# A gated three-tap convolution that reads its projection from PSUM: one core, layer trunk in float32 halves

## The reference

```python
def conv_ffn(h, w_up, w_dw, b_dw, w_down):        # w_up: 1024 -> 5632, w_dw: 3 taps a channel
    a = causal_dwconv(h @ w_up, w_dw) + b_dw
    g, val = jnp.split(a, 2, axis=-1)
    return (jax.nn.silu(g) * val) @ w_down
```

## Time and profile before

| | us |
|---|---|
| runs before the change: median (lowest to highest of 3) | 1390.86 (1390.37 to 1390.91) |
| the profiled execution, its own time | 1390.45 |
| its span, first to last instruction | 1388.7 |
| TensorE busy | 1279.1 |
| VectorE busy | 970.8 |
| ScalarE busy | 568.2 |
| GpSimd busy | 556.9 |
| mean granted TensorE clock | 0.963 |

### The profile page before, as it was taken

How to read it: one execution, slowest core, us unless ns; L and a number is a source line. 1 busy time by engine, 2 the same in 40 slices (tenths; PEclk the granted TensorE clock), 3 DMA queues, 4 the chain that set the end, 5 groups by cost and what they waited for, 6 DMA issues and landing times.

```text
span 1388.7 us, 17136 instructions
## 1 busy us (share of the span) xinstructions
PE 1279.1 (92%) x5496; PEld 998.6 (72%) x5496; DVE 970.8 (70%) x1309; ACT 568.2 (41%) x873; POOL 556.9 (40%) x265
## 2 busy tenths in 40 slices
PE   4899899889989889999999999989999999999996
PEld 2666676667667667778888767746778888887885
DVE  5667777773689899888734699985288988994102
ACT  3345555453533333334212364565344454442221
POOL 1332323213234343345444267772344444544440
PEclk9799999999989999999999999999999999999998
DMA  8533233332244444422444221110222322333221
GB/s 321 198 134 107 106 121 121 114 114 76 91 165 133 141 160 142 151 88 91 156 156 172 95 91 61 61 60 0 92 73 94 106 91 91 99 96 110 84 96 60
DMA packets 44918, 156.78 MB, mean 113 GB/s; under 512 B 4936, under 2 KB 5192, under 8 KB 44880
## 3 DMA queue, kind: packets, MB, share of 16 engines
q1 hardware_dynamic: 43488, 153.98, 32.6%
q10 hardware_dynamic: 1392, 2.32, 0.5%
HBM read 154.15 MB, written 2.12 MB: 113 GB/s over the span
## 4 chain that ended last, share of the span: by engine, by line
PE 69%; DVE 16%; issue 7%; ACT 5%; DMA 2%; DVEq 0%; SPq 0%; ACTq 0%
PE psum L834 20%; PE psum L835 20%; PE psum L836 20%; PE psum L1102 3%; DVE z L1305 2%; DMA ada_first<-ada_w 2%; DVE acc_mid L1184 2%; DVE tmp L1454 2%; PE psum L845 2%; DVE tmp L1226 2%; ACT L556 1%; DVE h_lo L1230 1%; DVE acc L1184 1%; DVE pt_lo L1314 1%; PE psum L881 0%
## 5 line engine op out<-in xcount | busy, mean ns | idle before, releaser
L454 POOL TENSOR_TENSOR w_lo<-w_raw,w_hi 128x1024 fp32r<-128x1024 f32 (+1 forms) x192 | 479.1, 2511 | 776.6 <-ACT w_hi L535 776.6
L834 PE MATMUL psum<-h_hi,w_hi 128*128 128x512 f32 x1152 | 477.4, 414 | 13.7 <-DVE h_lo L1230 8.5
L835 PE MATMUL psum<-h_lo,w_hi 128*128 128x512 f32 x1152 | 460.3, 400 | 0.0
L836 PE MATMUL psum<-h_hi,w_lo 128*128 128x512 f32 x1152 | 459.5, 399 | 0.0
L834 PEld LDWEIGHTS psum<-h_hi,w_hi 128*128 128x128 f32 x1152 | 223.8, 194 | 69.9 <-DVE h_lo L1230 11.1
L836 PEld LDWEIGHTS psum<-h_hi,w_lo 128*128 128x128 f32 x1152 | 223.1, 194 | 48.8
L835 PEld LDWEIGHTS psum<-h_lo,w_hi 128*128 128x128 f32 x1152 | 222.8, 193 | 48.0 <-issue 5.3
L535 ACT ACTIVATE w_hi<-w_raw 128x1024 fp32r<-128x1024 f32 (+1 forms) x192 | 191.6, 1037 | 84.1 <-DMA w_raw<-w_tiles 84.1
L1412 DVE SCALAR_TENSOR_TENSOR x<-psum,mod,x 128x512 f32<-128x512 f32 (+1 forms) x32 | 23.3, 749 | 180.5 <-PE psum L836 180.5
L834 PE MATMUL psum<-a_hi,w_hi 128*128 128x512 f32 x352 | 139.3, 396 | 0.8 <-issue 0.8
L836 PE MATMUL psum<-a_hi,w_lo 128*128 128x512 f32 x352 | 138.9, 395 | 0.0
(11 more groups left out here) (176 smaller groups left out, 1486.2 us busy)
## 6 DMA issues: line engine op xcount, KB each, us to landing
w_raw<-w_tiles SPq DMA_DIRECT2D x160, 512.0 KB, 3.4
ada_buf<-ada_w SPq DMA_DIRECT2D x32, 512.0 KB, 3.3
ada_mid<-ada_w SPq DMA_DIRECT2D x32, 512.0 KB, 3.5
w_raw<-w_tiles SPq DMA_DIRECT2D x32, 448.0 KB, 3.2
ada_first<-ada_w SPq DMA_DIRECT2D x16, 512.0 KB, 6.1
ada_late<-ada_w SPq DMA_DIRECT2D x16, 512.0 KB, 4.2
x<-x_in SPq DMA_DIRECT2D x4, 512.0 KB, 10.1
bias<-rel_scratch ACTq DMA_DIRECT2D x1, 2048.0 KB, 8.1
```

The costliest lines, as they stand in the source:

```text
L454: nc.gpsimd.tensor_tensor(w_lo[:, slot, 0:k], w_raw[:, (ph.tile + l) % 2, 0:k], f(w_hi[:, slot, 0:k]), ALU.subtract).then_inc(lo_done, 1)
L834: nc.tensor.matmul(dst, w_hi[:, slot, k], rhs_hi, start=first, stop=False)
L835: nc.tensor.matmul(dst, w_hi[:, slot, k], rhs_lo, start=False, stop=False)
L836: return nc.tensor.matmul(dst, w_lo[:, slot, k], rhs_hi, start=False, stop=last)
```

## The change

ScalarE no longer copies the banks to padded tiles. It applies tap 2 and the bias to each bank on the way (Identity with a scale and a bias column) into tap buffers that alternate with the group: `tmp0` and `tmp1` for c = 0, the bodies of `pad_g` and `pad_v` for c = 1. VectorE adds taps 1 and 0 to them, reading shifted columns of the PSUM banks. Silu goes back into bank 2c, the product is formed there in place, ScalarE rounds it from there into `a_hi`, and VectorE subtracts from there. ScalarE's two or three splits stand between these steps. Silu's table is loaded explicitly ahead of each body. TensorE waits for `act_ready` before it uses the banks again, and the zero columns are gone.

```diff
+        taps_g = (tmp0[:], pad_g[:, 2:S + 2])
+        taps_v = (tmp1[:], pad_v[:, 2:S + 2])
...
             def up_phase(ph, then, layer):
                 def group(i, c, nxt):
+                    w = [col("ff", lin(i, 8 * (FM * layer + c) + n, 16)) for n in range(8)]
+                    m = lin(i, c, 2)
                     act.wait_ge(used, lin(i, ph.group + c + 1, 2))
-                    act.wait_ge(taps_done, lin(i, FM * layer + c + 1, 2))
-                    nc.scalar.activation(pad_g[:, 2:S + 2], psum[:, 2 * c], ACT.Copy).then_inc(pad_ready, 1)
-                    nc.scalar.activation(pad_v[:, 2:S + 2], psum[:, 2 * c + 1], ACT.Copy).then_inc(pad_ready, 1)
-                    split_group(*nxt)
+                    if not (isinstance(i, int) and i == 0):
+                        act.wait_ge(act_ready, lin(i, FM * layer + c - 1, 2))
+                    nc.scalar.activation(taps_g[c], psum[:, 2 * c], ACT.Identity, bias=w[3],
+                                         scale=w[2]).then_inc(pad_ready, 1)
+                    nc.scalar.activation(taps_v[c], psum[:, 2 * c + 1], ACT.Identity, bias=w[7],
+                                         scale=w[6]).then_inc(pad_ready, 1)
+                    slots_free(nxt[0], nxt[1], nxt[2])
+                    split_tile(nxt[0], nxt[1], nxt[0].per_group * nxt[2])
                     act.wait_ge(conv_g, lin(i, FM * layer + c + 1, 2))
-                    nc.scalar.activation(tmp0[:], tmp0[:], ACT.Silu).then_inc(silu_done, 1)
-
-                with act.Fori(0, ph.bodies - 1) as i:
+                    nc.scalar.activation(psum[:, 2 * c], taps_g[c], ACT.Silu).then_inc(silu_done, 1)
+                    split_tile(nxt[0], nxt[1], nxt[0].per_group * nxt[2] + 1)
+                    act.wait_ge(gated, lin(i, FM * layer + c + 1, 2))
+                    nc.scalar.activation(tile_of(a_hi, m), psum[:, 2 * c], ACT.Copy).then_inc(a_hi_done, 1)
+                    for j in range(2, nxt[0].per_group):
+                        split_tile(nxt[0], nxt[1], nxt[0].per_group * nxt[2] + j)
+
+                load_table(ACT.Silu)
+                for c in range(2):
+                    group(0, c, (ph, 1, c))
+                with act.Fori(1, ph.bodies - 1) as i:
+                    load_table(ACT.Silu)
                     for c in range(2):
                         group(i, c, (ph, i + 1, c))
...
             def up0_pair(i, c):
-                pe.wait_ge(pad_ready, lin(i, 2 * (c - 1), 4))
+                pe.wait_ge(act_ready, lin(i, c - 1, 2))
                 pair(UP0, i, c)
...
-            V.memset(pad_g[:, 0:2], 0.0).then_inc(taps_done, 1)
-            V.memset(pad_v[:, 0:2], 0.0).then_inc(act_ready, 1)
...
-                    V.tensor_scalar(tmp0[:], pad_g[:, 2:S + 2], w[2], w[3], ALU.mult, ALU.add)\
-                     .then_inc(dve_step, own.tick())
+                    V.scalar_tensor_tensor(out=g[:, 1:S], in0=psum[:, 2 * c, 0:S - 1], scalar=w[1], in1=g[:, 1:S],
+                                           op0=ALU.mult, op1=ALU.add).then_inc(dve_step, own.tick())
...
+                    V.scalar_tensor_tensor(out=g[:, 2:S], in0=psum[:, 2 * c, 0:S - 2], scalar=w[0], in1=g[:, 2:S],
                                            op0=ALU.mult, op1=ALU.add).then_inc(conv_g, 1)
...
-                    V.tensor_tensor(tmp1[:], tmp0[:], tmp1[:], ALU.mult).then_inc(dve_step, own.tick())
-                    dve.wait_ge(dve_step, own.now())
+                    V.tensor_tensor(psum[:, 2 * c], psum[:, 2 * c], v, ALU.mult).then_inc(gated, 1)
+                    dve.wait_ge(a_hi_done, lin(i, FM * layer + c + 1, 2))
                     m = lin(i, c, 2)
-                    V.tensor_copy(tile_of(a_hi, m), tmp1[:]).then_inc(dve_step, own.tick())
-                    dve.wait_ge(dve_step, own.now())
-                    V.tensor_tensor(tile_of(a_lo, m), tmp1[:], f(tile_of(a_hi, m)), ALU.subtract)\
+                    V.tensor_tensor(tile_of(a_lo, m), psum[:, 2 * c], f(tile_of(a_hi, m)), ALU.subtract)\
                      .then_inc(act_ready, 1)
```

More of the change, by code:

```diff
@@ L270, in trunk @@
         o_copied, o_squared, ms_read, o_inv = sem("o_copied"), sem("o_squared"), sem("ms_read"), sem("o_inv")
-        pad_ready, silu_done = sem("pad_ready"), sem("silu_done")
+        pad_ready, silu_done, a_hi_done = sem("pad_ready"), sem("silu_done"), sem("a_hi_done")
         sig_ready, prod_ready = sem("sig_ready"), sem("prod_ready")
@@ L289, in trunk @@
         conv_g, taps_done, act_ready = sem("conv_g"), sem("taps_done"), sem("act_ready")
+        gated = sem("gated")
         u_ready, y_ready = sem("u_ready"), sem("y_ready")
@@ L1046, in group @@
                             if isinstance(i, int) and i == 0 and c == 0:
-                                pe.wait_ge(act_ready, FM * layer + n + 2)
+                                pe.wait_ge(act_ready, FM * layer + n + 1)
                             last = mm3(psum[:, 2 * c], 3 * c + j, k, a_hi[:, n], a_lo[:, n], n == 0, n == FM - 1)
@@ L1052, in down @@
                 for c in range(2):
-                    pe.wait_ge(pad_ready, 2 * (FM * (layer + 1) - 1 + c))
-                    if c == 1:
-                        pe.wait_ge(act_ready, FM * (layer + 1) + 1)
+                    pe.wait_ge(act_ready, FM * (layer + 1) - 1 + c)
                     group(0, c)
@@ L1145, in _ @@
             keep_warm(18)
-            pairs(UP1, 5 * DK, pad_ready, 2 * FM, 2)
+            pairs(UP1, 5 * DK, act_ready, FM, 1)
             group = down(DOWN1, 1)
@@ L1443, in group @@
                     dve.wait_ge(pad_ready, lin(i, 2 * (FM * layer + c) + 2, 4))
-                    dve.wait_ge(act_ready, lin(i, FM * layer + c + 1, 2))
-                    V.tensor_scalar(tmp1[:], pad_v[:, 2:S + 2], w[6], w[7], ALU.mult, ALU.add)\
-                     .then_inc(dve_step, own.tick())
+                    V.scalar_tensor_tensor(out=v[:, 1:S], in0=psum[:, 2 * c + 1, 0:S - 1], scalar=w[5],
+                                           in1=v[:, 1:S], op0=ALU.mult, op1=ALU.add).then_inc(dve_step, own.tick())
@@ L1447, in group @@
                     dve.wait_ge(dve_step, own.now(back=1))
[L1448 to L1452, removed]
@@ L1453, in group @@
-                    dve.wait_ge(dve_step, own.now(back=1))
-                    V.scalar_tensor_tensor(out=tmp0[:], in0=pad_g[:, 0:S], scalar=w[0], in1=tmp0[:],
+                    V.scalar_tensor_tensor(out=g[:, 2:S], in0=psum[:, 2 * c, 0:S - 2], scalar=w[0], in1=g[:, 2:S],
                                            op0=ALU.mult, op1=ALU.add).then_inc(conv_g, 1)
                     dve.wait_ge(dve_step, own.now())
-                    V.scalar_tensor_tensor(out=tmp1[:], in0=pad_v[:, 0:S], scalar=w[4], in1=tmp1[:],
-                                           op0=ALU.mult, op1=ALU.add).then_inc(taps_done, 1)
+                    V.scalar_tensor_tensor(out=v[:, 2:S], in0=psum[:, 2 * c + 1, 0:S - 2], scalar=w[4],
+                                           in1=v[:, 2:S], op0=ALU.mult, op1=ALU.add).then_inc(taps_done, 1)
@@ L1459, in group @@
                     dve.wait_ge(silu_done, lin(i, FM * layer + c + 1, 2))
[L1460 to L1462 removed]
+                    dve.wait_ge(taps_done, lin(i, FM * layer + c + 1, 2))
+                    V.tensor_tensor(psum[:, 2 * c], psum[:, 2 * c], v, ALU.mult).then_inc(gated, 1)
+                    dve.wait_ge(a_hi_done, lin(i, FM * layer + c + 1, 2))
@@ L1473, in up @@
                     mid_pieces(0, 1)
-                    own.loop(12)
+                    own.loop(4)
                     with dve.Fori(1, MID) as i:
```

2 lines of the change are left out of this document (1 added, 1 removed).

## The result

The changed kernel takes 1337.6 us, median of four runs (1335.82 to 1340.88), against 1390.88 (1390.37 to 1392.86) for the kernel before: a ratio of 0.9618 [0.9599, 0.9636]. Measured again beside the first experiments, five runs have a median of 1339.6 and a ratio of 0.9631 [0.9609, 0.9653].

What follows compares the result with a forecast made beforehand. TensorE's waits for VectorE's `acc_mid` in layer 0's up-projection were taken as the bound. Eight bodies going from 28.81 to 23.14 us (10.67 + 12.47) save 45.4: 1390.45 to 1345.0 us, range 1340 to 1362.

Steps and rivals of the forecast that it cites:

- What bounds the kernel: Layer 0's up-projection: TensorE waits 29.3 us in 8 times for VectorE's `acc_mid`; 47.8 us is all there is to win.
- PSUM-reading steps don't wait for GpSimd: VectorE's taps, with one PSUM and one SBUF input, take 0.75 us beside GpSimd's subtractions, against 2.88 now.
- The chain's steps: After T, when a projection group's two banks are done: Identity 0.80 us, taps 0.75, `act_ready` about T + 6.0.
- The chain's end: TensorE's load of `acc_mid` in layer 0: T + 10.67 against 14.11, T being when a group's two banks are done.
- 2.3 to 2.9 named as a sign: New profile: one `acc_mid` step per group takes 2.3 to 2.9 us, the collision with GpSimd having moved there.
- The floor of a body: Layer 0's body at TensorE's pace: 21.76 us plus 1.08 for the adaLN product, 22.84.
- Bodies of 28.81: Layer 0's up-projection before the change: 8 bodies from 384.33 to 614.81, 28.81 us each, forecast to become 23.14.
- The range: 1340 to 1362 us: from TensorE's floor with 47.8 saved and 3 for noise, up to most of rival B's 1353 to 1368.
- DMA, removed memsets, layer 1: nothing: Loads land with 3 to 4 us left, the removed memsets are off the path, layer 1 gains 0.
- Table loads: Loads of 1.28 us leave the chain, one explicit load per body stays; their gain is counted within the chain.
- The cost of held banks: Banks held until `act_ready` (6.0), wanted again 10.6 after T: 4.6 us of cover; anything past it is paid 44 times.
- rival C: Slower, banks held too long: each group 1.0 us late, 22 us in layer 1, 1413 to 1420 in all; chance 0.04.

## Where the prediction was right, and where it missed

The mechanism came out as forecast, and the time did not: 1337.6 lies below 1340 to 1362. The end of the chain was put too late, the floor of a body too high, and the range's allowance for scatter too small.

- **What bounds the kernel**: right. TensorE's wait for `acc_mid` in layer 0 was the whole of it, and 48.68 of 49.6 us came from that stretch; 47.8 had been called all there is to win.
- **PSUM-reading steps don't wait for GpSimd**: right. No such step of the changed kernel exceeds 0.753 in its 44 groups, and the taps from `x` in SBUF show 2.89 at the same place. The Trainium skill ("SBUF — State Buffer", Who interferes with whom) has the rule: a VectorE instruction with two SBUF inputs contends with a GpSimd instruction that reads SBUF, over a shared pair of ports that is an exclusive lock. The traces agree: 2.89 against 0.74, and the held tap from `x` (457.69) ends at 460.58, half a microsecond behind GpSimd's instruction (457.22 to 460.03). The Trainium skill's other rule, which spoke against the edit ("VectorE: DVE Perf Modes", Rules for kernel authors: copy out of PSUM first where many operations follow), would have lost the 36 us. The dearer PSUM source isn't seen in the taps, 0.75 against 0.74; it is seen in VectorE's other steps, 0.81 against 0.55 for `tensor_scalar` and 0.69 against 0.43 for the cast.
- **The chain's steps**: Identity 0.78 (0.80), taps 0.74 to 0.75 (0.75), `act_ready` at T + 6.05 (6.02).
- **The chain's end: the first missed term.** Predicted T + 10.67, measured 10.30. GpSimd's two subtractions ended at T + 7.24, not 7.5, since the VectorE steps beside them no longer hold it up either (4.77 for two, the lower of my two rows), and the held `acc_mid` step ended 0.55 behind them, not 0.7: 1.82 us long, below the 2.3 to 2.9 named as a sign. TensorE's weight loads follow each other without a gap up to 529.71: the lateness of 0.3 us a body, 2.4 us in eight, was not there.
- **The floor of a body: the second.** 21.76 + 1.08 = 22.84 was assumed, 22.71 measured (11.69 + 11.02): the adaLN product costs 0.95 here, not what it cost in DOWN0. 0.13 x 8 = 1.0 us. Both together are the 3.3 us between 45.4 and 48.68.
- **Bodies of 28.81**: the one worked through adds up to 14.11 + 13.81 = 27.92. The 0.9 between the two, 7.1 us in eight, is the first body (32.00) and the two of 29.5, and the prediction didn't say what would become of it. It went with the pauses; that this came out is luck as far as the working goes.
- **The range: the third.** Its lower end was TensorE's floor with 3 us more for noise, and three runs of the kernel before within 0.54 us had made noise look small. Nine later runs of that same kernel reach from 1386.23 to 1397.15. The changed kernel's first four spread over 5 us (1335.82 to 1340.88), the profiled one being the slowest; of its nine runs in all, six lie under 1340, and both medians do. The median before less the 48.68 is 1342.2; the other 4.6 down to 1337.6 lie around the stretch, where 3 had been allowed, and no run shows whether any of them are the change's.
- **DMA, removed memsets, layer 1: nothing**: right. Layer 1's body is unchanged. (A buffer free at 8.9 that lands 3.7 later lands by 12.6, not 12.4; nothing hung on it.)
- **Table loads**: worth nothing, as said, but for another reason. They were to leave the chain and gain there, and one a body was to stay. They had never stood in the chain, and none is left in the layer-0 bodies (15 between 380 and 600 in the trace before).
- **The cost of held banks** didn't come up, but its price "paid 44 times" was wrong: it is paid about once a body. By that, an estimate, rival C would have cost about half of what I gave it in layer 1.
- **What held what**: I priced the change as one. Added to the kernel before one after the other, the runs share the stretch's 48.68 out: taps from PSUM 33.4 us, the order of the splits 2.9, and product, difference and rounding from PSUM with the first tap on ScalarE the other 12.5, of which the first tap, taken back by itself, is 1.3. In another sequence the shares are others: taken back from the changed kernel, the taps' input is worth 7.0. Rounding on ScalarE, explicit table loads and doubled buffers are worth nothing each.

What stays open: what makes the start of layer 0's up-projection scatter between 379.8 and 384.4 from run to run. The granted clock ahead of it differs as well (0.93 for the start at 383.02, 0.94 for 380.94), but the two don't move together in every run, and which causes which was not tried. Product, difference and rounding were not moved to PSUM singly either.

## What to carry to other kernels

Where VectorE and GpSimd both stream through SBUF, look for VectorE steps whose time jumps by one GpSimd instruction (0.74 to 2.89 us here), and put one of the two inputs in PSUM: matmul output that is there already can stay, and a temporary can be sent there. Follow the whole chain, since a freed step moves the hold to the next one with two SBUF inputs, and what it saves is the difference between the two. Once TensorE is busy throughout a stretch (181.80 of 181.80), stop: a chain made shorter there gives nothing, as the run with the cut `acc_mid` steps shows.

## What was not expected of the hardware

- A held step shifts, and so costs less than its hold: 2.15 us at the tap lengthened the chain by 1.1, because `acc_mid` (4.18 before, 3.10 after) then met an idle GpSimd.
- GpSimd is slowed in turn: two subtractions take 4.76 to 4.77 us beside the changed kernel's PSUM-reading taps, 4.92 to 5.44 among the SBUF-reading ones of the kernel before, and 5.49 to 5.62 beside the taps from `x`.
- A stretch in which TensorE never waits repeats to 0.01 us (181.80 in nine profiles), while the phases ahead of it, with many short waits, scatter by up to 4.6 us.
- A PSUM input costs VectorE nothing in a `scalar_tensor_tensor` (0.75 against 0.74), but 0.26 us in a `tensor_scalar` (0.81 against 0.55) and in a cast (0.69 against 0.43).
- The clock followed the pauses: 0.91 over layer 0's up-projection before, 1.00 without them; with the 0.7 us pauses of the taps from SBUF no drop was seen, and with those of up to 1.6, 1.9 and 1.7 us (table above) the stretch had 0.99, 0.98 and 0.97. It was over a third of the gain: TensorE's busy time fell by 19.3 of the 48.68 us, and since eight pauses at clock 1.00 (taps from SBUF) add only 1.95 to it, some 17 are the clock's, an estimate.
